# The 65-row product of an implicit filter: from eight plain fp32 matmuls to three products each of rounded parts

## The reference, cut to what matters

```python
def hyena_filters(L, w1, b1, w2, b2, w3, b3, freq):
    ...
    h = jnp.sin(fr * (emb @ w1 + b1))          # (256, 64)
    h = jnp.sin(fr * (h @ w2 + b2))            # (256, 64)
    h = h @ w3 + b3                            # (256, 64) @ (64, 2048)
    ...
    window = jnp.exp(-t * jnp.abs(deltas))
    return h[:, :D_HY] * window, h[:, D_HY:] * window
```

## Time and profile before

| | |
|---|---|
| device time, median of 3 runs | 2271.89 us (2271.6 to 2272.32) |
| the profiled execution's own time | 2271.43 us |
| its span, first to last instruction | 2269.6 us |
| mean granted TensorE clock | 0.999 |
| PE busy | 2255.0 us, 99% of the span |
| DVE busy | 1675.8 us, 74% |
| ACT busy | 1331.4 us, 59% |

### The profile page before, as it was taken

One profiled execution on the slowest core, in us unless ns is written; L12 is line 12 of the kernel. 1 busy time (PEld: TensorE's weight loads), 2 busy tenths in 40 slices (PEclk: granted clock), 3 DMA queues, 4 the chain that ended last, 5 costly groups with the idle time before them and its releaser, 6 DMA issues.

```text
span 2269.6 us, 26632 instructions
## 1 busy us (share of the span) xinstructions
PE 2255.0 (99%) x10625; PEld 1874.2 (83%) x10625; DVE 1675.8 (74%) x2025; ACT 1331.4 (59%) x1775; POOL 105.2 (5%) x138
## 2 busy tenths in 40 slices
PE   9999999999999999999999999999999999999998
PEld 7778888888888888888888888888888888888887
DVE  6676864887778788787878788778788685456664
ACT  6455444766666666666666666666666564444443
POOL 0000000000000000000000000000000010000000
PEclk9999999999999999999999999999999999999999
DMA  9454455899998998996578999989988645644343
GB/s 356 167 172 165 165 186 186 279 292 272 287 307 262 275 293 267 283 282 238 221 279 241 287 289 260 285 281 275 275 278 258 240 148 219 243 176 149 149 162 117
DMA packets 77131, 542.63 MB, mean 239 GB/s; under 512 B 8681, under 2 KB 9012, under 8 KB 13967
## 3 DMA queue, kind: packets, MB, share of 16 engines
q1 hardware_dynamic: 61568, 429.58, 50.2%
q0 software_dynamic: 15296, 111.23, 22.8%
q10 hardware_dynamic: 144, 0.12, 0.0%
HBM read 534.60 MB, written 6.29 MB: 238 GB/s over the span
## 4 chain that ended last, share of the span: by engine, by line
PE 96%; DVE 2%; ACT 0%; issue 0%; ACTq 0%; POOLq 0%; POOL 0%
PE P L358 93%; PE P L361 3%; DVE low L625 1%; DVE R_f L610 0%; DVE R_f_r L610 0%; DVE R_h L613 0%; DVE X L613 0%; DVE R_g L613 0%; ACT R_h L501 0%; ACT hi L506 0%; ACT EV L532 0%; DVE st L613 0%; ACT EV L501 0%; DVE R_f L707 0%; ACT X L501 0%
## 5 line engine op out<-in xcount | busy, mean ns | idle before, releaser
L625 DVE TENSOR_TENSOR low<-raw,hi 128x1024 fp32r<-128x1024 f32 (+3 forms) x694 | 813.7, 1201 | 300.7 <-ACT hi L506 295.7
L506 ACT ACTIVATE hi<-raw 128x1024 fp32r<-128x1024 f32 (+3 forms) x694 | 704.4, 1040 | 467.1 <-PE P L358 299.2
L358 PE MATMUL P<-hi,R_h 128*128 128x512 f32 (+2 forms) x2944 | 944.1, 392 | 1.9 <-DVE low L625 1.5
L358 PE MATMUL P<-hi,R_f_r 128*128 128x512 f32 x2480 | 791.2, 391 | 0.1
L358 PEld LDWEIGHTS P<-hi,R_h 128*128 128x128 f32 x2944 | 552.5, 188 | 117.3 <-issue 6.1
L358 PE MATMUL P<-low,R_h 128*128 128x512 f32 (+2 forms) x1472 | 570.6, 388 | 0.0
L358 PEld LDWEIGHTS P<-hi,R_f_r 128*128 128x128 f32 x2480 | 465.8, 188 | 96.3 <-DVE R_f_r L610 0.3
L358 PE MATMUL P<-low,R_f_r 128*128 128x512 f32 x1240 | 482.8, 389 | 0.0
L625 DVE TENSOR_TENSOR low<-R_f,hi 128x1024 fp32r<-128x1024 f32 x226 | 267.6, 1222 | 82.3 <-ACT hi L506 81.4
L358 PEld LDWEIGHTS P<-low,R_h 128*128 128x128 f32 x1472 | 276.9, 188 | 54.4 <-issue 2.4
L358 PEld LDWEIGHTS P<-low,R_f_r 128*128 128x128 f32 x1240 | 233.0, 188 | 47.1
(11 more groups left out here) (229 smaller groups left out, 1406.2 us busy)
## 6 DMA issues: line engine op xcount, KB each, us to landing
raw<-in_w_d SPq DMA_DIRECT2D x128, 1024.0 KB, 7.1
R_f<-in_w_u POOLq DMA_DIRECT2D x84, 1024.0 KB, 10.4
raw<-in_w_u SPq DMA_DIRECT2D x72, 1024.0 KB, 5.4
raw<-in_w_z SPq DMA_DIRECT2D x45, 1024.0 KB, 4.8
raw<-in_w_i SPq DMA_DIRECT2D x36, 1024.0 KB, 4.9
R_f<-in_w_u SPq DMA_DIRECT2D x28, 1024.0 KB, 6.7
X<-in_w_u SPq DMA_DIRECT2D x28, 1024.0 KB, 9.0
raw<-in_w_mo SPq DMA_DIRECT2D x16, 1024.0 KB, 4.8
```

Of the source, the lines that this page charges most:

```text
L358: return self.e.matmul(o, l, r, start=start, stop=stop, skip_group_check=True)
L506: self.e.activation(hi, raw, ACT.Copy).then_inc(*self.inc("high_made", ("high", k, d)))
L625: self.e.tensor_tensor(low, raw, hi.bitcast(f32), ALU.subtract).then_inc(*self.inc("low_made", *lows))
```

## The change

Two more operand pairs are laid out: `w3_h`, `w3_l` and `h2_h`, `h2_l`. The low parts lie over the fp32 data from which they are made. `filter_3` issues three matmuls (high·high, high·low, low·high) in place of one plain fp32 matmul. Of the entries of `extra`, the one between `filter_2` and `sine_2` and the one behind `sine_2`, both empty before, now make the parts of w3, 1024 columns each; one new entry behind them makes the parts of h. It waits for both w3 entries, since their marks are in the same list `fl["h2"]`. So from `filter_3` on each entry comes one place later in `extra`.

```diff
+        self.w3_h, self.w3_l = self.R_mr[0:65, 2048:4096], R_fr[0:65, 6144:8192]
+        self.h2_h, self.h2_l = R_sr[0:65, 3456:3712], R_sr[0:65, 2688:2944]
...
-        self.mm(m.P[b][:, :], m.f_h2[:, 128 * t:128 * t + 128], m.f_w3[:, 512 * g:512 * g + 512], True, True
-                ).then_inc(*self.inc("turn_done", done))
+        o, t, g = m.P[b][:, :], slice(128 * t, 128 * t + 128), slice(512 * g, 512 * g + 512)
+        self.mm(o, m.h2_h[:, t], m.w3_h[:, g], True, False)
+        self.mm(o, m.h2_h[:, t], m.w3_l[:, g], False, False)
+        self.mm(o, m.h2_l[:, t], m.w3_h[:, g], False, True).then_inc(*self.inc("turn_done", done))
...
+    def w3_parts(q):
+        q = slice(1024 * q, 1024 * q + 1024)
+        fl["h2"].append(plain_parts(m.w3_h[:, q], m.w3_l[:, q], m.f_w3[:, q], fl["c"]))
+
+    def h2_parts():
+        fl["h2"] = [plain_parts(m.h2_h, m.h2_l, m.f_h2, list(fl["h2"]))]
...
-    extra += [load_bias, filter_1, nop, sine_1, nop, filter_2, nop, sine_2, nop]
+    extra += [load_bias, filter_1, nop, sine_1, nop, filter_2, lambda: w3_parts(0), sine_2, lambda: w3_parts(1), h2_parts]
```

## The result

The changed kernel takes 2277.36 us (median of 11 runs, 2276.29 to 2279.21), the kernel before 2271.98 on the same chip (11 runs, 2271.52 to 2273.38): a ratio of 1.0025, 95% interval 1.0017 to 1.0032, or 5.4 us more. The forecast was 2275.3 with an own range to 2276.3; the measured time lies outside that and inside the whole range (2271.5 to 2278.0). The profiled execution took 2276.29 us, its span 2274.5.

What follows compares the result with a forecast made beforehand. PE's stream of matmuls, busy 99% of the span, was taken as the bound. The terms -1.5 + 0.8 + 4.1 = +3.4 us gave a forecast of 2275.3 us, own range 2274.3 to 2276.3, whole range 2271.5 to 2278.0.

Steps and rivals of the forecast that it cites:

- Term 1: Filter products: eight plain fp32 matmuls each become three rounded ones at 0.227 us, a gain of 1.5 us.
- The other end of the range: Filter products: if a rounded matmul's price went with its 65 rows of contraction, a gain of 4.2 us.
- Term 2: End of gemm 2: ACT's copy of w3 ahead of the evacuation costs PE 0.8 us (0.3 to 0.9).
- The lower bound: Copy of w3 at gemm 2: 0.4 us if time counted in proportion to its 65 partitions.
- Term 3: End of gemm 5: filter_4's later sums delay ACT's k_parts copies and evacuation; PE loses 4.1 us (3.7 to 4.4).
- The edits at nothing: Other moved entries, such as h2_parts (0.6 us to spare), dft_parts and k_dft: no cost to PE.
- no gaps: Rival: moved lists don't hold evacuations up, only the products' gain is left, 2269.9 to 2270.4 us; chance 0.10.
- part of the gap: Rival: the gap behind gemm 5 is only 1 to 3 us, total 2273.2 us; chance 0.10.
- the clock's price: Behind the gap at gemm 5: a half-rate stretch like that at the kernel's start, costing +1.7 us.
- slower: Whole kernel: a time above 2276.4 us, beyond the 0.2% a measurement can tell from no change; chance 0.20.
- The forecast mechanism: Gains at the products, waits behind gemms 2 and 5, clock unchanged: +3.4 us in sum; chance 0.60.
- The rival: PE's clock falls to half rate in the 4.4 us gap behind gemm 5: 2277.0 us (2276.4 to 2278.7); chance 0.17.

Runs made afterwards that it cites:

- e7: Kernel before with the three rounded products, parts of w3 and h made in earlier entries so nothing behind moves: 2270.67 us, ratio 0.9994.
- e8: Kernel before with the three products, first half of w3's parts made at the end of gemm 2, nothing else moved: 2271.45 us, ratio 0.9998.
- e1: Kernel before with one more empty entry behind sine_2, plain fp32 products, no new parts: 2278.62 us, ratio 1.0027.
- e2: Changed kernel with filter_4 and the second dft_parts exchanged, putting filter_4 at its old place in DVE's list: 2272.02 us, ratio 0.9999.
- e3: Changed kernel with the last k_parts copy put behind gemm 5's evacuation: 2276.88 us, ratio 1.0022.
- e9: Kernel before with three products, early w3 and h parts, final empty entry left out so entries from filter_3 come half a tile earlier: 2270.45 us, ratio 0.9994.
- e6: Changed kernel with 12 more rounded matmuls on PE ahead of the transposes behind gemm 5: 2276.61 us, ratio 1.0019.

## Why the prediction was right, and where it was not

- **Term 1, forecast -1.5:** measured -1.46 in e7. The value of 0.227 for 65 rows held: a rounded matmul with 65 rows stands 0.23 us from the next, as one with 128 rows does, and not 0.12. The other end of the range (-4.2) fell.
- **Term 2, forecast +0.8:** measured +0.77 in the trace after and +0.80 alone in e8. The estimate that a copy of 65 partitions takes as long as one of 128 held: it took 1.04 us, and the next instruction started 0.95 behind its start. (The lower bound, in proportion, would be 0.95 x 65/128 = 0.48, not 0.4.) The Trainium skill ("ScalarE: Activation LUTs", "What ACT_TABLE_LOAD costs") gives 186 ns + 0.833 ns for each element of a lane with an overlap of about 93 ns between instructions, measured with 128 lanes. By its figures that is an estimate of 1.04 and 0.95 us for 1024 elements: the trace agrees, and shows it for 65 lanes too.
- **Term 3, forecast +4.1:** measured +4.35, and the same in e1, where it stands alone with the clock (6.75 - 2.37 = 4.38). Each link came where the prediction had it: low part, memset, sums, row, eight copies, evacuation, 0.14 us. The term was 0.2 too small because consecutive instructions of different kinds were put end to end: the low part starts 0.03 behind the conversion's end and takes 1.23 in place of 1.20, and the memset starts 0.15 behind the low part's end. That ACT and not DVE ends the wait is shown by the changed kernel and e2, where DVE's last part of the filters starts only when PE has gone on, and by e3, where it ended 1.2 us before. In the kernel before, DVE's ended just at PE's start (153.84 + 2.34 = 156.18), so that trace alone could not tell.
- **The edits at nothing:** held. No other wait appeared, and the stretch behind gemm 6 is as long in all kernels (2085.2 to 2085.6; 2086.0 in e9).
- **The other rivals fell.** Both gaps are there in full, so neither "no gaps" nor "part of the gap" came true, and the products do what the diff says.
- **What failed is the step that left the clock out of the sum.** The prediction worked the clock's price out (+1.7, 2277.0) but gave that case a chance of 0.17, because no row showed a gap as long. But its own term 3 brought the gap about wherever the forecast came true, and the only rows that bore on what such a gap does, those of the kernel's start, showed an array at half rate after standing still (by the distance of its loads; the granted clock in the windows reads 1.00 there). The clock cost 1.46 us in the profiled execution; the medians leave 5.4 - 3.7 = 1.7 for it. By all signs it did not fall only now and then: all 11 executions show a mean granted clock of 0.997 or 0.998, and none the 0.999 that 23 of 30 executions of the kernel before show. The rounded means can't prove it for each one. The chance of "slower" (over 0.2%) was set at 0.20, most of it this rival's. The kernel is 0.25% slower, and the interval reaches down to 0.17%, so on which side of that bound it lies stays undecided; that it is slower does not.

The forecast mechanism and the rival were not alternatives at all. The rival was a further term of the same chain.

What stays open is how long the clock stays down. The same gap cost 1.46 (after) and 2.37 (e1), a shorter one 2.40 (e3), with one profile for each. Open too is how often it falls behind a gap of 2 us (e6).

## What to carry to other kernels

When a change puts new entries into an order that is fixed at build time, price what it pushes back first: here the products gained 1.5 us, a copy put ahead of an evacuation lost 0.8, and the shifted list lost 4.35 and with the slow clock behind it 5.8. Look for the point where another engine's chain was just in time, count that chain's delay in full, and if the wait that comes of it is longer than any in the trace, add the price of the slow clock behind it to the sum rather than to the rivals. The new work belongs in entries that were empty and don't stand directly ahead of something that TensorE waits for; and if a wait can't be avoided, fill it whole.

## What the runs showed of the hardware that was not expected

In the profiled execution of e6 the clock fell behind an idle time of 1.96 us, from 157.57 to 159.52, with matmuls at the full rate on both sides; in some of its other executions it seems to have held. In the kernel before, the longest idle time behind the warm-up, 1.59 us at 1826.4, left it at 1.00:

```profile
1828.01 1.32 PE L361 MATMUL P<-ident,X 128*128 128x128 f32 x8 [1.59 <-DVE X L613]
```

The window that holds most of this wait, and the next one:

```profile
1826.00:1828.00 2.00, 0.42 (x2) 0.00 (x0) 1.90 (x7) 0.00 (x0) 0.59 (x1) 1.00 0.27 41
1828.00:1830.00 2.00, 1.76 (x10) 1.28 (x11) 2.00 (x6) 1.51 (x5) 0.00 (x0) 1.00 0.86 328
```

The Trainium skill ("TensorE: Matmul & The Clock Gate", "HAM oscillation — how this bites in real kernels") warns of long idle stretches between bursts; the traces agree in kind, and show a fall behind one of 2 us, and that filling a part of a gap may save nothing. The prediction had named this section and still kept the clock out of its sum. The fall need not come within the gap either: in the changed kernel the clock was down when PE resumed, in e6 only behind the transposes.
